# Router weights made one stage earlier, and two weight loads held back behind a row gather, in a two-layer hybrid backbone kernel

## What the reference computes

```python
def route(h, router_w, router_bias):
    scores = jax.nn.sigmoid((h @ router_w).astype(jnp.float32))
    ...
    _, top_idx = lax.top_k(masked, MOE_TOP_K)          # 8 of 64 experts
    w = jnp.take_along_axis(scores, top_idx, axis=1)
    return top_idx, w / jnp.sum(w, axis=-1, keepdims=True) * ROUTED_SCALE

def moe_ffn(h, ...):
    ...   # assignments sorted by expert, gathered, one expert's weights per block of rows
    yb = lax.map(lambda a: swiglu(a[0], w_gate[a[1]], w_up[a[1]], w_down[a[1]]), (xb, blk_exp))
    yb = yb.reshape(P, D) * buf_w[:, None]
    routed = jnp.zeros((N + 1, D), yb.dtype).at[buf_tok].add(yb)[:N]
    return swiglu(h, s_gate, s_up, s_down) + routed
```

## Time and profile before

| | before |
|---|---|
| median of 3 runs | 3226.75 us (3226.22 to 3231.83) |
| the profiled execution | 3225.9 us, span 3224.0 us |
| PE busy | 2859.1 us (89%) |
| DVE busy | 1498.2 us (46%) |
| ACT busy | 848.9 us (26%) |
| POOL busy | 869.0 us (27%) |
| DMA | 723.88 MB, mean 225 GB/s |

### The profile page before, as it was taken

How to read it: one execution, slowest core, us unless ns; L and a number is a source line. 1 busy time by engine, 2 the same in 40 slices (tenths; PEclk the granted TensorE clock), 3 DMA queues, 4 the chain that set the end, 5 groups by cost and what they waited for, 6 DMA issues and landing times. The chain is left out here.

```text
span 3224.0 us, 57706 instructions
## 1 busy us (share of the span) xinstructions
PE 2859.1 (89%) x20700; PEld 1440.4 (45%) x20701; DVE 1498.2 (46%) x2940; ACT 848.9 (26%) x1565; POOL 869.0 (27%) x882
## 2 busy tenths in 40 slices
PE   6998897979979999999977998979888889877896
PEld 3644675864533333333323554758844223222231
DVE  3433644754544444444445434537644434333344
ACT  2222542122222222222224223431122222212222
POOL 0020004431033444444434010025211433322234
PEclk8998998999999999999988998989899899888997
DMA  9300440023439999999968102300136699999966
GB/s 381 139 8 30 161 151 7 4 100 115 163 143 351 391 383 377 368 418 410 373 241 303 47 30 84 134 15 4 69 115 248 244 415 416 417 417 417 417 237 241
DMA packets 139220, 723.88 MB, mean 225 GB/s; under 512 B 30368, under 2 KB 48288, under 8 KB 102304
## 3 DMA queue, kind: packets, MB, share of 16 engines
q1 hardware_dynamic: 84800, 544.15, 42.9%
q0 software_dynamic: 33792, 102.80, 8.8%
q10 hardware_dynamic: 20448, 74.46, 5.7%
HBM read 619.62 MB, written 101.71 MB: 224 GB/s over the span
## 5 line engine op out<-in xcount | busy, mean ns | idle before, releaser
L2312 PE MATMUL psum<-arena 128*64 x1792 | 832.6, 618 | 98.3 <-DVE arena L2410 98.3
L2314 PE MATMUL psum<-arena 128*64 128x512 f32 x1792 | 832.5, 618 | 0.0
L2288 POOL DMA_INDIRECT arena<-h,arena x456 | 501.0, 1099 | 838.5 <-DVE arena L1602 714.3
L2312 PEld LDWEIGHTS psum<-arena 128*64 128x64 f32 x1792 | 244.0, 141 | 599.1 <-issue 599.1
L2334 PE MATMUL psum<-arena 128*64 x896 | 406.8, 596 | 13.0 <-DVE arena L2417 13.0
L831 PE MATMUL psum<-arena 128*128 128x480 f32 (+3 forms) x1088 | 403.6, 526 | 16.3 <-PEq L167 8.0
L2336 PE MATMUL psum<-arena 128*64 128x512 f32 x896 | 407.0, 597 | 0.0
L831 PEld LDWEIGHTS psum<-arena 128*128 128x128 f32 x1088 | 207.0, 194 | 191.5 <-issue 179.2
L2362 ACT ACTIVATE arena<-psum 128x256 f32<-128x256 f32 x112 | 43.2, 386 | 917.8 <-PE psum L2314 917.8
L2377 ACT COPY arena<-arena 128x2048 f32 x114 | 217.0, 1903 | 125.1 <-DMA arena<-in_w_gu 110.3
L2314 PEld LDWEIGHTS psum<-arena 128*64 128x64 f32 x1792 | 243.8, 141 | 0.0
(11 more groups left out here) (357 smaller groups left out, 3933.0 us busy)
## 6 DMA issues: line engine op xcount, KB each, us to landing
arena<-in_w_gu SPq DMA_DIRECT2D x130, 2048.0 KB, 17.5
arena<-in_w_dn SPq DMA_DIRECT2D x130, 1024.0 KB, 15.6
y_slots<-arena ACTq DMA_DIRECT2D x122, 512.0 KB, 9.3
arena<-in_ada SPq DMA_DIRECT2D x24, 2048.0 KB, 8.1
y_slots<-arena SPq DMA_DIRECT2D x4, 4096.0 KB, 27.5
arena<-in_w_gdn SPq DMA_DIRECT2D x6, 1536.0 KB, 9.3
arena<-in_w_out SPq DMA_DIRECT2D x2, 4096.0 KB, 14.1
arena<-in_w_tok SPq DMA_DIRECT2D x4, 1920.0 KB, 7.6
```

The lines of the kernel that those rows point to most:

```text
L2288: nc.gpsimd.indirect_dma_start(xg[:, u % 2, b], None, h2_quads, bass.IndirectOffsetOnAxis(ap=idx[:, u, b:b + 1], axis=0)).then_inc(gathere ...
L2312: nc.tensor.matmul(psum[half(0), 2 + r, :], xT[:, r, rows_of(k, 0)], W[:, bass.ds(at + k * 2 * DE, 2 * DE)], start=(k == 0), stop=(k == DK ...
L2314: last = nc.tensor.matmul(psum[half(1), 2 + r, :], xT[:, r, rows_of(k, 1)], late_gu[:, k * 2 * DE:(k + 1) * 2 * DE], start=(k == 0), stop= ...
```

## The change

In `phase_tail` DVE makes the weights of tiles 2 to nq-1 ahead of its wait for `hot_used` (before: tiles 4 and 5 in layer 0, none in layer 1), and those of tiles 0 and 1 after the plan's last small operation, ahead of its wait for `gathered[0]`. In `phase_experts` the weights of tiles 0 to 3, which stood between `turn_rows(1)` and `product(0)`, are gone, with their chain semaphore `step`. SP waits for `gathered[0]` before it issues the down loads of experts 3 and 4. No operation is added or dropped.

```diff
@@ phase_tail, SP
                         sp.wait_ge(dn_prod, nq)
+                        sp.wait_ge(gathered[0], 16 * QUADS)
                         load_dn(LOW)
                         load_dn(LOW + 1)
@@ phase_tail, DVE
-                        for i in range(NLT, nq):
+                        for i in range(2, nq):
                             token_weights(ch, i, wk, route_keep)
                         dve.wait_ge(hot_used, nq)
@@
+                        for i in range(2):
+                            token_weights(ch, i, wk, route_keep)
                         dve.wait_ge(gathered[0], 16 * QUADS)
                         turn_rows(0, xg, xT).then_inc(xT_ready, 1)
@@ phase_experts, DVE
-                        ch = Chain(dve, step)
                         at = slot(dve, 0, 1)
                         copy_gu(None, at)
                         later = later_pairs(dve)
                         copy_dn(None, at)
                         dve.wait_ge(gathered[1], 16 * QUADS)
                         turn_rows(1, xg, xT).then_inc(xT_ready, 1)
-                        for i in range(NLT):
-                            token_weights(ch, i, wk, route_keep)
                         e, at = late_expert(dve, 1), slot(dve, 1, 1)
                         product(0, 0)
```

More of the change, by code:

```diff
@@ L2216, in phase_experts @@
                 y_out = [S("y_out0"), S("y_out1")]
-                step = S("step")
                 units_done = S("units_done")
```

## The result

| | before | after |
|---|---|---|
| median, 4 runs each | 3229.29 us (3226.22 to 3232.52) | 3205.31 us (3202.57 to 3206.45) |
| ratio, 95% interval | | 0.9924 (0.9907 to 0.9942) |
| profiled execution, span | 3225.9, 3224.0 us | 3205.58, 3203.7 us |

The medians differ by 24.0 us; the prediction was 23.1. The interval of the ratio allows 19 to 30.

A forecast was written before the change was run, and what follows sets the result against it. PE was taken to bound layer 0, DMA layer 1 once the ring's lead is used up. Layer 0's 8.36 + 2.19 - 0.3 = 10.2 and layer 1's 4.28 + 6.74 + 1.92 = 12.9 gave 23.1 us: 3203.6 us, range 3198.5 to 3213.

The forecast's parts named there:

- Weights out of the stage: Expert stage start: unit 0's product waits for SiLU alone, 8.36 us sooner in layer 0, 6.74 us in layer 1.
- the first rival: Layer 1's DMA bound eats the gain from weights and clock; 14.5 us left, 3212.2 us; chance 0.12.
- The clock: Second unit's gate and up products: PE's clock holds through short idle, saving 2.19 us in layer 0, 1.92 in layer 1.
- The third rival: The clock falls all the same in the second unit, giving 3207.8 us; chance 0.12.
- The earlier landing: Layer 1, first unit's gathered rows: land 4.28 us sooner with down loads held back; bound 4.8 us with no contention.
- the contention: Last two gather issues beside two tiles' weights: each 0.25 us longer, so rows land 0.5 us later.
- the 2.5 to 3 us named as a sign of being right: Layer 1: first unit's rows should land this long behind the last gather issue's end.
- the 2.47 us taken for the landing: Layer 0's time from the last gather issue's end to the first unit's rows landing, assumed for layer 1 too.
- the 0.3 us charged in layer 0: Layer 0: cost of the 0.5 us later landing, partly covered by SP loads and ACT's last store.
- the second rival: GpSimd's gather issues are shut out while DVE makes two tiles; gain 15.6 us, 3211.2 us; chance 0.08.
- The waits as cover: Waits for `gathered[0]` and `hot_used` hide the moved weights, 4.32 us per two tiles; no cost at the `hot_used` wait.
- perhaps another 1.5: Layer 1's `gate_up(0)`: a shorter slow stretch might give this many us more, counted in the range only.

The follow-up runs named there:

- The weights alone: Changed kernel without SP's wait for the gathered rows, so only the token weights are moved: 3211.74 us against 3229.28 for the kernel before.
- all tiles at the first wait: Changed kernel with all tiles' weights ahead of the wait for `hot_used`, none at the gather's wait: 3210.63 us against 3230.23 for the kernel before.
- the load wait alone: Kernel before with only SP's wait for the gathered rows added, token weights left in place: 3224.74 us against 3229.28.
- the two kernels with the tiles placed otherwise: Changed kernel with weights of tiles 0 to 3 at the gather's wait, 3211.3 us; with all tiles ahead of the `hot_used` wait, 3210.63 us.
- fillers: Changed kernel plus unread matmuls on TensorE ahead of the first unit and DVE's register loads for unit 1 moved earlier: 3202.94 us against 3230.23 before.
- the kernel with seven fillers: Kernel before plus 7 unread matmuls on TensorE between unit 0's gate and up products and its hidden-row turning: 3231.41 us against 3230.23.

## Why the prediction was right

- **Weights out of the stage**, forecast 8.36 and 6.74 us: the time from SiLU to product fell by 8.39 and 6.78 us. The weights alone gave 17.5 us, so the first rival (layer 1's DMA bound eats its share) is refuted. That the loads behind follow PE is borne out by the last stretch of 692 to 696 us in every trace.
- **The clock**, forecast 2.19 and 1.92 us: 2.20 and 1.91 in the first profile. Right in size, but less certain than I put it: of the six profiled executions with the weights moved, all had `gate_up(1)` in 7.15 us in layer 0, but two (weights alone, all tiles at the first wait) had 8.84 us in layer 1. The third rival is therefore real for single executions, at 1.7 us. The prediction's sum asked only how long PE would be idle; its third rival named that PE has been slow before. In the two where the clock fell, the first unit had taken 10.01 and 9.75 us, the longest of the twelve; in the ten where it held, 7.1 to 9.5 us. So what the engine ran like before the gaps may count as well; no run tests this.
- **The earlier landing**, forecast 4.28 us with a bound of 4.8: 4.79 us, and 4.96 with the load wait alone, a little over the bound. The step that was missized is the contention: I charged 0.5 us of landing for two issues lengthened by 0.25 us each. In the traces one issue of the two is longer, by 0.48 us, but the landing follows by 0.2 us only (4.96 against 4.79 in layer 1, 10.12 against 10.31 in layer 0): the rows then land 2.0 us behind the last issue's end, under the 2.5 to 3 us named as a sign of being right, and 2.2 to 2.5 without the weights in layer 0. Why the landing does not follow in full is open. The rest is the 2.47 us taken for the landing, which was 2.29 with the load wait alone. Of the 0.3 us charged in layer 0 about 0.2 is seen; that 10.26 stands beside 10.29 is the chance of one trace, since 10.29 is the highest of the five without weights there.
- **The port.** The Trainium skill ("SBUF — State Buffer", section "Who interferes with whom") calls the shared port pair an exclusive lock, for which a VectorE operation with two SBUF inputs contends with a GpSimd instruction that reads SBUF; it also says that in a probe `tensor_tensor` and `tensor_reduce` did not stall DMA. The traces lie between the two: in each layer one issue, started 0.08 us behind the first of DVE's operations, is longer by 0.48 us, less than one operation of 0.69, and the next keeps its length. A single turn lost would be compatible with that; no run shows what held it. A lock-out over all six operations, the second rival, did not occur, not with four tiles beside the issues either.
- **The waits as cover**, forecast nothing: right, and the two kernels with the tiles placed otherwise lost 6.0 and 4.2 us, where the covers left over had said 7 to 8 (the traces: 7.3) and 4.
- **What the sum left out.** The first unit's own slow stretch: in layer 0 the first SiLU came 0.88 us later than before, in layer 1 it came 0.85 us sooner than the landing explains. The prediction named a shorter slow stretch in layer 1 in its range ("perhaps another 1.5") and not in its sum, and layer 0's nowhere. The 0.88 us is no doing of the edit as far as the traces tell: with the rows turned at the same time, the first SiLU of layer 0 stood 24.4 to 25.3 us behind the anchor over eight profiles, and at 25.17 in one where no weights were moved. By layer the forecast was 10.2 and 12.9 us and the traces have 9.7 and 14.3, so the errors of -0.5 and +1.4 partly cancel, and 23.1 against 24.0 looks better than its parts. That is luck. In layer 1 fillers took 2 us of that slow stretch back. What decides on which side of it an execution falls was not settled.

## What to carry to other kernels

Work that nobody waits for until much later (here weights that only the last phase reads) belongs into waits of its engine, and each wait holds just what its idle time says: the idle column of the timeline forecast the cost of each placement tried to within 2 us. A bulk load released at the same moment as a small gather that the next stage waits for is worth holding back until the gather has landed, if it is itself needed late (4.96 us here). In a stage bound by DMA whose requests are released by compute, a stall of compute at its start still cost its full length here.

## What was not expected of the hardware

- The granted clock fell to 0.50 in the second unit although TensorE's gaps before it were only 0.9 us each (in two of the twelve second units with the weights moved, both behind a first unit of 9.75 us or more). It rose at different points of the first unit from run to run: without fillers ahead of it its gate and up products took 8.5 to 10.1 us.
- With a gap of 2.9 us behind work at a clock of 1.00 it fell to 0.50 as well (both layers of the kernel with seven fillers).
- A 128x128 by 128x512 matmul in f32 took two passes of 0.43 us, so a filler costs 0.86 us at the high clock.
